# Gate and up products of four feed-forward parts by seven block products instead of eight, with the weight sums on GpSimd

## The reference, cut to what matters

```python
D_FF = 2816
def swiglu(x, w_gate, w_up, w_down):
    return (jax.nn.silu(x @ w_gate) * (x @ w_up)) @ w_down

for l in range(DEPTH_2):      # DEPTH_2 = 2
    x = x + 0.5 * swiglu(rms_norm(x, norm_ffn1[l]), ffn1_w_gate[l], ffn1_w_up[l], ffn1_w_down[l])
    x = x + hybrid_mixer(rms_norm(x, norm_mix[l]), w_in[l], ...)
    x = x + 0.5 * swiglu(rms_norm(x, norm_ffn2[l]), ffn2_w_gate[l], ffn2_w_up[l], ffn2_w_down[l])
```

## Time and profile before

| | |
|---|---|
| median of 3 runs | 2646.37 us (2644.08 to 2647.72) |
| the profiled execution | 2642.54 us, its span 2640.7 us |
| TensorE products, busy | 2556.0 us, 97% of the span |
| TensorE weight loads, busy | 2063.1 us, 78% |
| VectorE, busy | 1312.9 us, 50% |
| ScalarE, busy | 930.7 us, 35% |
| GpSimd, busy | 201.1 us, 8% |
| loads from HBM | 276 MB, mean 109 GB/s |
| feed-forward parts, about | 463 to 727, 1121 to 1382, 1548 to 1812, 2265 to 2532 us |

### The profile page before, as it was taken

How to read it: one execution, slowest core, us unless ns; L and a number is a source line. 1 busy time by engine, 2 the same in 40 slices (tenths; PEclk the granted TensorE clock), 3 DMA queues, 4 the chain that set the end, 5 groups by cost and what they waited for, 6 DMA issues and landing times. The chain is left out here.

```text
span 2640.7 us, 31200 instructions
## 1 busy us (share of the span) xinstructions
PE 2556.0 (97%) x12661; PEld 2063.1 (78%) x12661; DVE 1312.9 (50%) x1708; ACT 930.7 (35%) x1262; POOL 201.1 (8%) x162
## 2 busy tenths in 40 slices
PE   7997996999999999999999999999999999999998
PEld 7876775788888878778888888888887777888886
DVE  5456996534345443654343454444543446544444
ACT  4344883322233234542222332222412255322222
POOL 0002112400003300100000000000050001000000
PEclk9998998999999999999999999999999999999999
DMA  4116994222224321223222232222332213232222
GB/s 147 57 56 234 408 387 149 92 96 96 96 82 132 102 72 54 76 88 96 92 93 95 88 104 96 93 98 89 119 108 87 66 35 102 88 100 92 96 94 74
DMA packets 88869, 292.37 MB, mean 111 GB/s; under 512 B 11522, under 2 KB 16530, under 8 KB 88466
## 3 DMA queue, kind: packets, MB, share of 16 engines
q1 hardware_dynamic: 81634, 264.10, 30.0%
q0 software_dynamic: 6224, 23.60, 2.3%
q10 hardware_dynamic: 864, 2.62, 0.2%
HBM read 276.12 MB, written 12.58 MB: 109 GB/s over the span
## 5 line engine op out<-in xcount | busy, mean ns | idle before, releaser
L496 PE MATMUL bank_l<-xg_hi,w_hi 128*128 128x512 f32 (+1 forms) x2144 | 841.4, 392 | 16.1 <-DVE w_lo L462 16.1
L496 PE MATMUL bank_l<-xg_lo,w_hi 128*128 128x512 f32 (+1 forms) x2144 | 838.8, 391 | 0.0
L496 PE MATMUL bank_l<-xg_hi,w_lo 128*128 128x512 f32 (+1 forms) x2144 | 834.4, 389 | 0.0
L462 DVE TENSOR_TENSOR w_lo<-w_raw,w_hi 128x1024 fp32r<-128x1024 f32 (+2 forms) x424 | 506.3, 1194 | 301.6 <-ACT w_hi L457 300.2
L457 ACT ACTIVATE w_hi<-w_raw 128x1024 fp32r<-128x1024 f32 (+2 forms) x424 | 427.6, 1010 | 445.4 <-PE bank_l L496 424.9
L496 PEld LDWEIGHTS bank_l<-xg_hi,w_hi 128*128 128x128 f32 x2144 | 403.6, 188 | 113.8 <-DVE w_lo L462 15.3
L496 PEld LDWEIGHTS bank_l<-xg_lo,w_hi 128*128 128x128 f32 x2144 | 402.9, 188 | 90.4 <-issue 2.2
L496 PEld LDWEIGHTS bank_l<-xg_hi,w_lo 128*128 128x128 f32 x2144 | 404.1, 188 | 87.5
L496 PE MATMUL bank_l<-hid_hi_ff,w_lo 128*128 128x512 f32 x704 | 280.9, 399 | 0.0
L496 PE MATMUL bank_l<-hid_lo_ff,w_hi 128*128 128x512 f32 x704 | 277.4, 394 | 0.0
L496 PE MATMUL bank_l<-hid_hi_ff,w_hi 128*128 128x512 f32 x704 | 276.0, 392 | 0.0
(11 more groups left out here) (386 smaller groups left out, 2531.9 us busy)
## 6 DMA issues: line engine op xcount, KB each, us to landing
w_raw<-in_ff_gate SPq DMA_DIRECT2D x88, 512.0 KB, 3.4
w_raw<-in_ff_up SPq DMA_DIRECT2D x88, 512.0 KB, 3.5
expert_raw<-in_experts SPq DMA_DIRECT2D x81, 512.0 KB, 19.2
w_raw<-in_in SPq DMA_DIRECT2D x80, 512.0 KB, 3.4
w_raw<-in_ff_down SPq DMA_DIRECT2D x64, 512.0 KB, 3.4
w_raw<-in_out SPq DMA_DIRECT2D x24, 512.0 KB, 3.5
w_raw<-in_ff_down SPq DMA_DIRECT2D x32, 384.0 KB, 3.0
w_raw<-in_experts SPq DMA_DIRECT2D x15, 512.0 KB, 20.1
```

Of the source, the lines that this page charges most:

```text
L462: dve.tensor_tensor(lo, panel_memory(i), hi.bitcast(F32), ALU.subtract).then_inc(*panel_lo.done(i))
L496: done = pe.matmul(dst, w[:, c * cols:(c + 1) * cols], moving, start=c == 0 and n == 0, stop=c == kc - 1 and n == 2)
```

## The change

**The algebra.** For a hidden tile j the gate panel (above) and the up panel (below) are read as a 2x2 matrix A of blocks: 2 x 128 hidden features by 2 x 512 features of x. x is a 2x2 matrix B of 2 x 512 features by 2 x 256 tokens. Strassen's method in Winograd's form gives A B with seven products of blocks. With S1 = A21 + A22, S2 = S1 - A11, S3 = A11 - A21, S4 = A12 - S2 and T1 = B12 - B11, T2 = B22 - T1, T3 = B22 - B12, T4 = B21 - T2 the products are A11 B11, A12 B21, S2 T2, S3 T3, S1 T1, A22 T4 and S4 B22, each with a contraction of 512 (4 chunks), 3 products of parts a chunk and 256 columns. Up has its own products no more: the halves of gate and up are sums of the seven.

**Which pairs.** `SEVEN_FROM` gives the first j that goes this way: 8 in `ff1_0`, 2 in the other three parts; so 14 + 3 x 20 = 74 pairs of 88. The pairs before it, and all down products, keep their products.

**The engines.** GpSimd, in a new `feed_forward_pool` placed before the mixer's part or behind it in its queue, writes the quarters of x back together (high + low part) and two of the four T; then, for each pair, the four sums S1, S3, S2, S4 of 128x512 numbers, into a single buffer `ws_raw`. VectorE forms T1 and T2. ScalarE rounds and VectorE takes remainders of the four T once a part, and of S3 with S2 and of S1 with S4 (128x1024 each) in each pair. Of an up panel only the half A22 is still split. ScalarE copies A11 B11 from PSUM to SBUF, since an operation of VectorE takes one PSUM operand here; VectorE then puts the seven together in four additions. `val` and the gate value have one buffer each instead of two, and silu works in place. Up panels have an own ring of two (`up_raw`). The loads of a slot whose occupant went by seven products also wait for GpSimd's last read of it (S3 for up, S4 for gate).

The diff, cut to its core:

```diff
+SEVEN_FROM = {f"ff{f}_{l}": FF_GROUPS[0] if (f, l) == (1, 0) else 2 for f in (1, 2) for l in range(DEPTH_2)}
...
-            gated = sb(phase, "gated_ff", [P, 2, T])
-            silu = sb(phase, "silu_ff", [P, 2, T])
-            val = sb(phase, "val_ff", [P, 2, T])
+            worked = sb(phase, "worked_ff", [P, 6, T // 2])
+            val = sb(phase, "val_ff", [P, T])
+            xs_hi = sb(phase, "xs_hi", [P, 4, DC // 2, T // 2], F32R)
...
+            up_raw = sb(phase, "up_raw", [P, UP_RAW, PANEL])
+            ws_raw = sb(phase, "ws_raw", [P, 4, PANEL // 2])
...
+                if by_seven(before):
+                    stage, n, which = by_seven(before)
+                    sp.wait_ge(*w_sums.upto((stage, n, "S3" if which == "up" else "S4")))
...
+        def piece(pe, stage, j, name, weights, moving):
+            for c in range(DC // 2):
+                for n, (w, m) in enumerate(((weights[0], moving[0]), (weights[0], moving[1]), (weights[1], moving[0]))):
+                    done = pe.matmul(product_at[name], w[:, c * P:(c + 1) * P], m[:, c, :], start=c == 0 and n == 0,
+                                     stop=c == DC // 2 - 1 and n == 2)
+            return done
...
+            emptied(seeded, "A11 B11")
+            signal(piece(pe, stage, j, "A11 B11", gate_half(pe, stage, j, 0), plain_x(0, 0)), "A11 B11")
+            emptied(together, "first")
+            piece(pe, stage, j, "A12 B21", gate_half(pe, stage, j, 1), plain_x(1, 0)).then_inc(*used.done(panel_of[gate]))
+            signal(piece(pe, stage, j, "S2 T2", sum_weights(pe, stage, j, "S2"), sum_x(pe, stage, "T2")), "S2 T2")
+            emptied(together, "up")
+            signal(piece(pe, stage, j, "S3 T3", sum_weights(pe, stage, j, "S3"), sum_x(pe, stage, "T3")), "S3 T3")
+            signal(piece(pe, stage, j, "S1 T1", sum_weights(pe, stage, j, "S1"), sum_x(pe, stage, "T1")), "S1 T1")
+            pe.wait_ge(*panel_lo.upto(panel_of[up]))
+            piece(pe, stage, j, "A22 T4", split_memory(panel_of[up]), sum_x(pe, stage, "T4")).then_inc(
+                *used.done(panel_of[up]))
+            emptied(together, "gate")
+            signal(piece(pe, stage, j, "S4 B22", sum_weights(pe, stage, j, "S4"), plain_x(1, 1)), "S4 B22")
...
+                def weight_sum(name, a, b, op):
+                    k = SUMS.index(name)
+                    if j > SEVEN_FROM[stage]:
+                        pool.wait_ge(*ws_low.upto((stage, j - 1, k // 2)))
+                    pool.tensor_tensor(ws_raw[:, k, :], a, b, op).then_inc(*w_sums.done((stage, j, name)))
+
+                pool.wait_ge(*panel_in[slot_of_panel[up]].upto(up))
+                weight_sum("S1", a21, a22, ALU.add)
+                pool.wait_ge(*panel_in[slot_of_panel[gate]].upto(gate))
+                weight_sum("S3", a11, a21, ALU.subtract)
+                pool.wait_ge(*w_sums.upto((stage, j, "S1")))
+                weight_sum("S2", ws_raw[:, SUMS.index("S1"), :], a11, ALU.subtract)
+                pool.wait_ge(*w_sums.upto((stage, j, "S2")))
+                weight_sum("S4", a12, ws_raw[:, SUMS.index("S2"), :], ALU.subtract)
...
+        def seven_act(act, stage, g, i, j):
+            up = panel_of[ff_keys(stage, j)[1]]
+            first, more = by_seven_first(stage, j), by_seven_next(stage, j)
+            round_sums(act, stage, j, 1)
+            take_first(act, stage, j)
+            if not first:
+                silu_act(act, stage, j - 1)
+            round_upto(act, up + 1)
+            round_upto(act, up + 2)
+            if not first:
+                hidden_act(act, stage, g, i - 1, j - 1)
+            if more:
+                round_sums(act, stage, j + 1, 0)
+            else:
+                silu_act(act, stage, j)
+                hidden_act(act, stage, g, i, j)
...
+        def seven_dve(dve, stage, i, j):
+            up = panel_of[ff_keys(stage, j)[1]]
+            first, more = by_seven_first(stage, j), by_seven_next(stage, j)
+            if not first:
+                gate_of_seven(dve, stage, j - 1)
+            rest_of_sums(dve, stage, j, 1)
+            if not first:
+                gate_times_up(dve, stage, j - 1)
+                scale_hidden(dve, stage, j - 1)
+            rest_upto(dve, up + 1)
+            first_and_common(dve, stage, j)
+            rest_upto(dve, up + 2)
+            if not first:
+                rest_of_value(dve, (stage, j - 1), hid_lo[:, i - 1, :], hid_hi[:, i - 1, :], val[:, :])
+            if more:
+                rest_of_sums(dve, stage, j + 1, 0)
+            common_and_more(dve, stage, j)
+            up_of_seven(dve, stage, j)
+            if not more:
+                gate_of_seven(dve, stage, j)
+                gate_times_up(dve, stage, j)
+                scale_hidden(dve, stage, j)
+                rest_of_value(dve, (stage, j), hid_lo[:, i, :], hid_hi[:, i, :], val[:, :])
```

More of the change, by code:

```diff
@@ L364, in gain, with by_seven @@
             return gains[:, g * DC + c:g * DC + c + 1]
-        slot_of_panel, before_in_slot, occupant, n_ring, n_expert = {}, {}, {}, 0, 0
+        def by_seven(i):
+            name, j = order[i]
+            if name[0:2] == "ff" and name[4:-2] in ("gate", "up"):
+                stage = name[0:3] + name[-2:]
+                if j >= SEVEN_FROM[stage]:
+                    return stage, j, name[4:-2]
+            return None
+        slot_of_panel, before_in_slot, occupant, n_ring, n_expert, n_up = {}, {}, {}, 0, 0, 0
         expert_panels = [i for i in range(len(order)) if order[i][0] == "experts"]
@@ L373, in build @@
                     place = ("raw", place[1] - EXPERT_OWN)
+            elif by_seven(i) and by_seven(i)[2] == "up":
+                place, n_up = ("up", n_up % UP_RAW), n_up + 1
             else:
@@ L387, in build @@
         panel_in = {("raw", r): steps(f"raw_arrived{r}", 16) for r in range(RAW)}
+        panel_in.update({("up", r): steps(f"up_arrived{r}", 16) for r in range(UP_RAW)})
         panel_in.update({("expert", r): steps(f"expert_arrived{r}", 16) for r in range(EXPERT_OWN)})
@@ new lines, in x_quarter, with scratch, by_seven_next, by_seven_first @@
+        def x_quarter(part, k, t):
+            return part[:, 4 * k:4 * k + 4, META + half_t * t:META + half_t * t + half_t]
+        def scratch(k, t):
+            return x_scratch[:, 4 * k:4 * k + 4, half_t * t:half_t * t + half_t]
+        x_sum_at = {"T1": (scratch(0, 0), 2), "T2": (scratch(1, 1), 1), "T3": (scratch(0, 1), 0), "T4": (scratch(1, 0), 3)}
+        def by_seven_next(stage, j):
+            return j + 1 not in (FF_GROUPS[0], FF_GROUPS[0] + FF_GROUPS[1], sum(FF_GROUPS))
+        def by_seven_first(stage, j):
+            return j == SEVEN_FROM[stage] or not by_seven_next(stage, j - 1)
@@ new lines, in take_first, with silu_act @@
+        def take_first(act, stage, j):
+            act.wait_ge(*seventh.upto((stage, j, "A11 B11")))
+            if j > SEVEN_FROM[stage]:
+                act.wait_ge(*together.upto((stage, j - 1, "first")))
+            act.activation(worked[:, 5, :], product_at["A11 B11"], ACT.Copy).then_inc(
+                *seeded.done((stage, j, "A11 B11")))
+        def silu_act(act, stage, j):
+            act.wait_ge(*taken.upto(ff_keys(stage, j)[0]))
+            act.activation(gate_value, gate_value, ACT.Silu).then_inc(*func.done((stage, j)))
+            if j == sum(FF_GROUPS) - 1:
+                load_log_and_exp(act)
@@ L1807, in feed_forward_act, with rest_of_sums @@
                     round_ahead(act, ff_down(stage, g, m))
+                    if g < len(FF_GROUPS) - 1 and m == DC - 2:
+                        round_sums(act, stage, j, 0)
                     if g == len(FF_GROUPS) - 1:
                         after_x(act, stage, m, g_next, before)
+        def rest_of_sums(dve, stage, j, pair):
+            both = slice(2 * pair, 2 * pair + 2)
+            dve.wait_ge(*ws_high.upto((stage, j, pair)))
+            dve.tensor_tensor(ws_lo[:, both, :], ws_raw[:, both, :], ws_hi[:, both, :].bitcast(F32),
+                              ALU.subtract).then_inc(*ws_low.done((stage, j, pair)))
@@ new lines, in x_sum_2, with twice, first_and_common @@
+        def x_sum_2(dve, stage):
+            dve.wait_ge(*quarter.upto((stage, "T3")))
+            dve.tensor_tensor(scratch(1, 1), scratch(1, 1), scratch(0, 0), ALU.subtract).then_inc(
+                *x_sums.done((stage, "T2")))
+        def twice(v):
+            return v.to_broadcast([P, 2, half_t])
+        def first_and_common(dve, stage, j):
+            if j > SEVEN_FROM[stage]:
+                dve.wait_ge(*taken.upto(ff_keys(stage, j - 1)[1]))
+            dve.wait_ge(*seeded.upto((stage, j, "A11 B11")))
+            dve.wait_ge(*seventh.upto((stage, j, "S2 T2")))
+            dve.tensor_tensor(worked[:, 0:3:2, :], halves[:, 0:2, :], twice(worked[:, 5:6, :]), ALU.add).then_inc(
+                *together.done((stage, j, "first")))
@@ new lines, in common_and_more, with up_of_seven @@
+        def common_and_more(dve, stage, j):
```

(11 more changed lines are left out.)

196 lines of the change are left out of this document (172 added, 24 removed).

## The result

| | before | after |
|---|---|---|
| median | 2646.99 us of 4 run beside it (2644.08 to 2647.72) | **2749.24 us** of 4 (2749.1 to 2749.37) |
| span of the profiled execution | 2640.7 us | 2747.3 us |

The account below looks back on a forecast made before the run. TensorE bounded the kernel before; VectorE and GpSimd alternating on SBUF would bound it after. Groups 49 us plus starts 12 us gave +61 on 2642.5, and with the median 3.8 us above the profiled execution 2707 us; range 2612 to 2755.

Parts of the forecast that it names:

- What bounds before, and a block product's cost: Feed-forward pairs: TensorE alone sets the pace at 11.12 us; a 256-column product costs 0.118 us, 84 take 9.9 us.
- VectorE's load and the layout of the pair: Steady pair: VectorE's twelve steps sum to 8.94 us, GpSimd's sums block it 3.67 us, so the period is 12.6 us.
- rival C: Steady pair: GpSimd's sums hold the ports longer, period 13.3 to 14.1 us, time 2743 to 2785 us; 8%.
- rival B: Steady pair: GpSimd's sums do not hold VectorE and TensorE stays the bound, time 2574 us; 12%.
- The groups' ends: First and last pairs of each group: +5.8 us for eight pairs, +2.8 or +4.2 for six; all groups together 49 us.
- the start of a part: x sums before the first S2 T2: ready about 25 us, due at 21; 4 us for three parts, nothing in the first.
- a rival on the clock: Gaps of 2 to 3 us within each period lower TensorE's clock; this is D, 4%.
- the forecast's formula: Group of n pairs: 10.8 + (n - 2) x 12.6 + 13.2 us, less TensorE's ready down-product chunks, 4.85 or 3.46.
- the forecast case: The main forecast for the whole kernel, period 11.8 to 13.4 us, time 2665 to 2749 us; 57%.
- A: Rival for the steady pair: sums slide under VectorE's PSUM steps and idle time, 52 periods lose 1.65 us, time 2621 us; 15%.
- D: Rival for the steady pair: clock falls in each period's gap, 84 products take 18 us, time 2847 us; 4%.

Follow-up runs that it names:

- experiment 2: Changed kernel with each of GpSimd's four weight sums replaced by filling one constant column (whole block in a part's first pair), so results are wrong: 2612.07 us, ratio 0.9873.
- Experiment 1: Changed kernel with each weight sum on GpSimd replaced by three constant fills that read no SBUF operand: 2660.25 us, ratio 1.0055.
- Experiment 3: Changed kernel with the four weight sums moved from GpSimd into VectorE's own queue: 2676.66 us, ratio 1.0118.
- 4: Changed kernel with seven products from pair 4 in the later parts, x sums still in pairs 0 and 1 (first part: pairs 4 and 5): 2740.38 us.
- 8: Changed kernel with seven products from the fourth pair (ninth in the first part), the four T made one at a time over three pairs: 2724.53 us, ratio 1.0302.
- 10: Kernel with 49 pairs in runs of at most three, weight sums on VectorE and led starts, given T3, T4 on VectorE and later first-part x sums: 2604.84 us.
- Kernel 11: Kernel 8 with T3 and T4 made on VectorE as well, and the first part's x sums one pair later: 2708.92 us, ratio 1.024.
- kernel 9: Kernel with 49 pairs in runs of at most three and led, spread-out starts, its weight sums on GpSimd instead of VectorE: 2660.77 us, ratio 1.0055.

## Why the prediction was right, and where it was off

**What bounds before, and a block product's cost:** right. 0.119 us measured against 0.118, and experiment 2 has the pair at 9.96 us against 9.9.

**VectorE's load and the layout of the pair:** right in each part. Blocked time 0.97 + 1.10 + 0.50 + 1.10 = 3.67 us forecast, at four named steps; 0.98, 1.09, 0.50 and 1.08 at the same four measured. Period 12.6 us forecast, 12.58 to 12.61 measured. Experiment 1 shows that GpSimd holds VectorE only when it reads: without its reading the same steps are not held. Experiment 3 shows the 8.94 us of load, since four more steps of 0.60 give 11.33. That a sum holds VectorE for 1.10 us and not for its whole 1.285 came out too, which ends rival C.

**A chain that the prediction left out** did no harm here, but is a bound of its own: experiment 1 has the chain over GpSimd and ScalarE at 11.02 us when each sum takes 1.64 us and nothing is blocked. With three sums of 1.285 us on it, it would be 11.02 - 3 x 0.355 = 9.95 us (my estimate from these numbers), just TensorE's own pair; so rival B needed this chain short as well as the ports free. The 2 to 3 us that TensorE stands in each period are there too, in pieces: products that should start 0.12 us apart start 1.63, 0.67 and 0.36 us apart (at 626.30, 630.78 and 635.71), and with the slower start behind each that makes the 2.6 us between 9.99 and 12.6.

**The groups' ends:** right. A group of eight in the middle costs (93.46 + 46.37) - (88.96 + 44.80) = 6.1 us, forecast 5.8; one of six at the end (68.29 + 36.05) - (66.72 + 33.61) = 4.0, forecast 4.2 (5.5 in the first part, where the clock was low for 3.4 us of its down products).

**The step that failed is the start of a part:** "I take 4 us for three parts (between 0 and 10), nothing in the first". A later part costs 27.3 us instead of 2.8 + 5.8 + 4.2 + 4 = 16.8. All of the difference is at its start: 15.5 to 15.9 us before the first down product, less the 1.6 us by which six such pairs are longer than six plain ones in a last group (68.3 against 66.7), is 14 us where I had 4. The gap is 11.6 of them. In the first part the "nothing" was 6.3 us, of it a gap of 3.7. So the starts make 30 + 6 us of the 46 by which the span is over the forecast, and 6.7 us are the late first product of the first part and the low clock behind it, which no term of mine could hold. In the median 4 us fewer show, for it lies at the profiled execution here and not 3.8 us above it.

What I missed was the order of the queues. I summed the work (about 25 us against a due time of 21): but T2 belongs to pair 1 in VectorE's order, whatever is ready, the weight sums stand behind T4, and the rounding stands behind a hidden value. That gave 11.6 us, over the 10 of my bound. In the first part eight plain pairs do not cover the x sums either, for they were put into the last two of them. I also priced a gap alone and not the clock, which fell to 1.2 GHz in it and stayed there for 10 to 14 us, 3 to 6 of them with products to do. How much that costs is less sure: some 2.4 us of each start lie behind the gap, but about the same in the fourth part, with 3 us of products at the low clock, as in the third with 6. I had a rival on the clock, but only for the gaps within a period, where it never fell.

Experiments 4, 8, 10 and 11 change the start and bear this out. Shifting the start by itself gives little while the x sums hold VectorE up (4); with the sums taken apart the gap shrinks to 4.7 us (8), and without GpSimd's T3 and T4 to about 2 us (11). Kernel 11, the change with another start, takes 2709 us, or 2713 with the 4.4 us of the three pairs that it has fewer: near the 2707 of the forecast, whose start cost 4 us. Its first groups, with their down products, are still 6 to 8 us longer than before, where the forecast's formula gives 1.3 us for five such pairs: gaps of about 2 us with 3.4 us of low clock behind them are in that; what the rest is stays open.

The range held although this step failed, because the other terms came out: for all groups but their starts 49 us were forecast and 51 measured. The time is at the upper edge of the forecast case (2749), and it got there by a cost that no rival has; that it is still inside the range is partly luck.

**Rivals.** A (the sums slide under PSUM steps), C and D did not happen. B's condition, no hold by GpSimd, was made by hand in experiment 2, and gave 2612 us, where B had 2574: of the 38 us between them the three later starts are some 27, and the first part's start, which B had at nothing, 6.6.

## What to carry to other kernels

Before work is moved to GpSimd, list VectorE's operations with two SBUF inputs beside it: here an addition over 512 cost VectorE 0.5 to 1.1 us, 3.65 us for the four, and doing them on VectorE cost 4 x 0.60 = 2.4. A method that saves 1.16 us in 11.12 us of TensorE's time pays only if every start of it is fed ahead, so lay out the first round of each stretch in queue order, and look at the clock behind a gap. With a plain pair in every four for the lagging engine, the sums back on VectorE and the starts fed ahead, the same algebra went from +3.9% to -1.6%; with the sums on GpSimd the plain pairs and a led start left +0.55% (kernel 9).
